# Dense feed-forward block: up products with the weights stationary and the tokens moving, results feature-major, no transposes of them

## The reference, cut to what matters

```python
D_MODEL, SEQ, D_FF = 1024, 256, 2816

def swiglu(u, w1, w3, w2):                 # u: 256 x 1024
    return (jax.nn.silu(u @ w1) * (u @ w3)) @ w2

# w1, w3: 1024 x 2816 (the two up products), w2: 2816 x 1024 (the down product)
```

## Time and profile before

| what | value |
|---|---|
| median of 3 runs | 2342.64 us (2339.24 to 2343.55) |
| span of the profiled execution | 2338.5 us |
| the profiled execution's own time beside its span | not listed; the shortest timed run is 0.7 us above the span |
| TensorE busy | 2098.2 us, 90% of the span |
| ScalarE, VectorE, GpSimd busy | 16%, 21%, 5% |
| the dense feed-forward (first up matmul to first matmul of what follows) | 357.23 to 598.87 us |

### The profile page before, as it was taken

One profiled execution on the slowest core, in us unless ns is written; L12 is line 12 of the kernel. 1 busy time (PEld: TensorE's weight loads), 2 busy tenths in 40 slices (PEclk: granted clock), 3 DMA queues, 4 the chain that ended last, 5 costly groups with the idle time before them and its releaser, 6 DMA issues. The chain is left out here.

```text
span 2338.5 us, 29578 instructions
## 1 busy us (share of the span) xinstructions
PE 2098.2 (90%) x12194; PEld 954.0 (41%) x12194; DVE 499.3 (21%) x1278; ACT 379.3 (16%) x878; POOL 116.4 (5%) x275
## 2 busy tenths in 40 slices
PE   5999998999999899999999999687798879879886
PEld 2574543444676343222222222154432328443232
DVE  2043841000159220000000011012311122131113
ACT  2022431000341321000000010022110010121011
POOL 2000000000000000000000000000000000000000
PEclk9999999999999999999999999887899899889999
DMA  9231359342673579999999999940899982079993
GB/s 319 93 123 45 136 182 329 134 146 90 238 266 132 219 280 362 412 407 398 408 402 412 404 406 411 373 151 0 326 422 422 422 314 73 36 317 422 422 418 148
DMA packets 192023, 644.22 MB, mean 275 GB/s; under 512 B 11635, under 2 KB 44875, under 8 KB 156043
## 3 DMA queue, kind: packets, MB, share of 16 engines
q1 hardware_dynamic: 165440, 469.92, 52.7%
q0 software_dynamic: 25824, 172.09, 18.1%
q10 hardware_dynamic: 619, 0.23, 0.0%
HBM read 641.15 MB, written 1.05 MB: 275 GB/s over the span
## 5 line engine op out<-in xcount | busy, mean ns | idle before, releaser
L1366 PE MATMUL bank<-ring,wide 128*32 128x512 f32 x3520 | 412.2, 598 | 22.2 <-DMA ring<-in_l_moe_w 20.6
L1403 PE MATMUL bank<-dreg,RB 128*32 128x512 f32 x2592 | 312.2, 601 | 7.4 <-DMA dreg<-in_l_moe_w 4.6
L1366 PEld LDWEIGHTS bank<-ring,wide 128*32 128x32 f32 x3520 | 108.6, 110 | 276.3 <-issue 245.1
L1349 PE MATMUL bank<-ring,wide 128*32 128x512 f32 x1472 | 189.0, 631 | 28.7 <-DMA ring<-in_w_up 27.3
L974 PE MATMUL bank<-wide,ring 128*128 128x256 f32 x832 | 182.1, 381 | 0.6 <-ACT wide L1808 0.6
L2945 DVE TENSOR_TENSOR H<-SG,bank 128x256 f32<-128x256 f32 x82 | 34.7, 423 | 689.6 <-ACT SG L2057 689.6
L974 PEld LDWEIGHTS bank<-wide,ring 128*128 128x128 f32 x832 | 158.5, 191 | 24.1 <-issue 2.2
L964 PE MATMUL bank<-ring,wide 128*128 128x512 f32 x352 | 158.2, 609 | 1.1 <-DMA ring<-in_w_kv 0.9
L1403 PEld LDWEIGHTS bank<-dreg,RB 128*32 128x32 f32 x2592 | 79.5, 110 | 190.7 <-issue 180.5
L1273 PE MATMUL bank<-ring,wide 128*128 128x512 f32 x352 | 154.6, 592 | 0.9 <-ACT wide L1808 0.9
L2972 DVE TENSOR_TENSOR TOK<-bank,TOK 128x512 f32<-128x512 f32 x84 | 57.9, 692 | 307.7 <-PE bank L1425 164.4
(11 more groups left out here) (445 smaller groups left out, 1617.7 us busy)
## 6 DMA issues: line engine op xcount, KB each, us to landing
ring<-in_l_moe_w SPq DMA_DIRECT2D x120, 1024.0 KB, 16.1
dreg<-in_l_moe_w POOLq DMA_DIRECT2D x88, 1024.0 KB, 8.5
dreg<-in_w_down POOLq DMA_DIRECT2D x64, 1024.0 KB, 12.8
ring<-in_w_gate SPq DMA_DIRECT2D x56, 1024.0 KB, 14.9
ring<-in_w_up SPq DMA_DIRECT2D x56, 1024.0 KB, 18.8
ring<-in_l_mod_w SPq DMA_DIRECT2D x24, 2048.0 KB, 8.2
ring<-in_l_moe_w SPq DMA_DIRECT2D x40, 768.0 KB, 12.7
ring<-in_l_ffn_w SPq DMA_DIRECT2D x22, 1024.0 KB, 10.0
```

The costliest lines, as they stand in the source:

```text
L1349: mm = pe.matmul(banks[r % 2][32 * g:32 * g + 32, :].rearrange("p (w n) -> p w n", w=2), tokens_of(m.order[i][0], c, k), w, start=k == 0, ...
L1366: mm = pe.matmul(banks[r % 3][32 * g:32 * g + 32, :].rearrange("p (w n) -> p w n", w=2), tokens_of(m.order[i][0], c, k), quads[:, s, :, k ...
L1403: mm = pe.matmul(banks[4 + 2 * m.lane(m.unit(m.order[i][0])) + h][32 * g:32 * g + 32, :], HQ[:, r % 4, j, 32 * q:32 * q + 32], dring[:, i ...
```

## The change

The up products swap their operands. A step is now one piece of work for all 256 tokens: with a 128x128 piece of the weights stationary and the 256 columns of `T1` moving, a matmul gives 128 features by 256 tokens. Four such groups of 8 matmuls fill two banks: the gate in bank `first`, the up part in bank `first + 1`. Steps alternate between banks 0, 1 and banks 2, 3. The result is feature-major, as the down product needs it, so the two transposes, ScalarE's copy and the two semaphores `turned_h` and `hidden_turned` go. ScalarE takes one silu of 128x512 per step, as soon as the gate's bank is full; VectorE multiplies 128x512 and writes to `H` in even steps, to `HT` in odd ones. `SG`, `H` and `HT` keep their memory and are seen as 512 columns. The down products of step st - 1 (8 matmuls, both token tiles) now follow the up products of step st. SyncE's code is not touched.

```diff
+                def up(st):
+                    s, first = st % RING, 2 * (st % 2)
+                    pe.wait_ge(sem(f"pair_in{s}"), 32 * (st // RING + 1))
+                    if st >= 2:
+                        pe.wait_ge(sem("hidden"), st - 1)
+                    for w in range(2):
+                        for j in range(2):
+                            for k in range(KC):
+                                operand_chunk(k, st == w == j == 0)
+                                m = pe.matmul(banks[first + w][:, j * T:(j + 1) * T], ring[:, s, k, (2 * w + j) * P:(2 * w + j + 1) * P],
+                                              T1[:, k, :], start=k == 0, stop=k == KC - 1)
                         m.then_inc(sem("upped"), 1)
...
+                def down(st):
+                    s = st % RING
+                    pe.wait_ge(sem(f"down_in{s}"), 16 * (st // RING + 1))
+                    pe.wait_ge(sem("hidden"), st + 1)
+                    for t in range(TT):
                         for j in range(2):
                             for n in range(2):
-                                m = pe.matmul(banks[4 + 2 * t + n][:, :], HT[:, t, j, :], dring[:, s, j, n * NCH:(n + 1) * NCH],
+                                m = pe.matmul(banks[4 + 2 * t + n][:, :], hidden_cols[st % 2][:, j * T + t * P:j * T + (t + 1) * P],
+                                              dring[:, s, j, n * NCH:(n + 1) * NCH],
                                               start=st == 0 and j == 0, stop=st == NSTEP - 1 and j == 1)
                         m.then_inc(sem("down_done"), 1)
-                    if 1 <= i <= nu:
-                        t = (i - 1) % TT
-                        pe.wait_ge(sem("hidden"), i)
-                        if i >= 3:
-                            pe.wait_ge(sem("hidden_turned"), i - 2)
-                        for j in range(2):
-                            m = pe.transpose(banks[2 + t][:, j * P:(j + 1) * P], H[:, t, j * P:(j + 1) * P], ident[:, :])
-                        m.then_inc(sem("turned_h"), 1)
+
+                for st in range(NSTEP):
+                    up(st)
+                    if st:
+                        down(st - 1)
+                down(NSTEP - 1)
...
+            for st in range(NSTEP):
+                act.wait_ge(sem("upped"), 2 * st + 1)
+                if st:
+                    act.wait_ge(sem("hidden"), st)
+                act.activation(silu_cols, banks[2 * (st % 2)][:, :], ACT.Silu).then_inc(sem("silued"), 1)
...
+            for st in range(NSTEP):
+                dve.wait_ge(sem("silued"), st + 1)
+                dve.wait_ge(sem("upped"), 2 * st + 2)
+                if st >= 2:
+                    dve.wait_ge(sem("down_done"), TT * (st - 1))
+                dve.tensor_tensor(hidden_cols[st % 2], silu_cols, banks[2 * (st % 2) + 1][:, :], ALU.mult).then_inc(sem("hidden"), 1)
```

More of the change, by code:

```diff
@@ L459, in two_blocks @@
         HT = sb("HT", [P, 2, 2, P])
+        silu_cols = SG[:, :, :].rearrange("p a n -> p (a n)")
+        hidden_cols = (H[:, :, :].rearrange("p a n -> p (a n)"), HT[:, :, :, :].rearrange("p a j n -> p (a j n)"))
         pairs = ring[:, :, :, :].rearrange("p s (w k) n -> p s w k n", w=2)
@@ L1259, in dense_ffn @@
             def dense_ffn():
[L1262 to L1274, removed]
-                        m.then_inc(sem("upped"), 1)
[L1276 to L1281, removed]
+                def up(st):
[9 more added lines that the diff above has]
+                                              T1[:, k, :], start=k == 0, stop=k == KC - 1)
+                        m.then_inc(sem("upped"), 1)
```

## The result

The changed kernel took 2325.0 us (median of 6 runs, 2317.43 to 2332.0) against 2343.1 us (6 runs, 2339.24 to 2347.48). The ratio is 0.9930, with a 95% interval of 0.9912 to 0.9947. The forecast was 2328.6 us and 14.0 us less. The profiled execution has a span of 2328.0 us, 10.5 us less than the one of before and 3.5 us more than the 2324.5 forecast for it. It belongs to a run of 2329.6 us, 4.6 us above the changed kernel's own median, so its span understates the gain.

A forecast was written before the change was run, and what follows sets the result against it. TensorE's own work was taken to bound the feed-forward; 4.84 + 8.49 + 1.44 + 0.20 - 0.8 - 0.2 = 13.97 us less, so 2342.64 - 14.0 gives 2328.6 us. The range was 2322 to 2337 us.

The forecast's parts named there:

- What bounds the stage: Feed-forward: TensorE's own work sets its length, busy 235.3 of 241.7 us, not the weights' supply or small engines.
- Transposes: Feed-forward units on TensorE: 22 transpose pairs of 0.22 us go, saving 4.84 us.
- The wait and the slow clock behind it: Before the first down product: 5.48 us idle for down weights and 3.01 us at half clock go, 8.49 us.
- Up products: Feed-forward up matmuls: 704 records of 256 columns at 0.2158 us, weight loads hidden, cost 0.8 us more.
- Start: First up group: TensorE may catch up with ScalarE's chunks, costing 0.2 us, between 0 and 0.9.
- Waits at the end: Last down units: waits for ScalarE's transpose copies (0.73 + 0.71 us) and the last unit's extra 0.20 us go.
- Rival C: Up products: weight loads from a ring slot being filled are not hidden, adding 48 us, time 2377; chance 4%.
- Handed on whole: Behind the feed-forward: later loads move with the chain, so the 14 us reach the end whole.
- within 3 us: Sign to check: the stretches behind the feed-forward stay as long as before to 3 us.

The follow-up runs named there:

- the late load: Changed kernel with SyncE issuing the first step's down weights last of the first four: stage 236.40 us, median 2329.95 us, ratio 0.9956.
- the second set: The changed kernel timed again without further edits: stage 227.65 us, median 2323.64 us, ratio 0.9924.
- the early load: Changed kernel with the first down weights issued behind the second pair of up weights: stage 227.65 us, median 2324.65 us, ratio 0.9926.
- the early table: Changed kernel with a one-column square root on ScalarE behind the last silu, loading its function table early: median 2322.70 us, ratio 0.9917.
- the control: The kernel before, unchanged, timed as if it were another kernel: stage 241.72 us, median 2341.39 us, ratio 0.9997.

## Why the prediction was right, point by point

- *What bounds the stage*: TensorE's own work. Confirmed: it is busy for all of it. The forecast of the stage (227.6 us) came out at 227.65 by this mechanism and not by luck: its two large terms were tested one by one.
- *Transposes* (4.84 us): 4.83 measured by putting them back.
- *The wait and the slow clock behind it* (8.49 us): 8.47 measured in the kernel before by issuing one load earlier. The margin was put at 1.4 us and is 1.0 in one trace and 1.4 in the other. That it decides is shown by the late load (+8.75 us).
- *Up products* (+0.8 us): 0.07 us per 64 records, and 0.9 us of up work more in the kernel before with its matmuls cut. The number was right; the reason given for it was not. The prediction said that a load of 0.191 us is hidden under a pitch of 0.2158 "with 25 ns to spare". At 128 columns records with a load each lie 0.112 us apart, so a load costs at most that, and at least 0.1 us was to spare.
- *Start* (+0.2 us): the first 128 records take 384.23 - 356.53 = 27.70 us where 2 x 13.81 = 27.62, so 0.08.
- *Waits at the end* (1.44 and 0.20 us): gone; the last down records run at 6.87 us a step and the next job follows. Not tested apart from the rest, but with the other terms measured, 13.99 - 4.83 - 8.47 + 0.7 + 0.1 = 1.5 us is left for them.
- *Rival C*, the one on the slower side, was rightly held unlikely, but neither its reason nor its price holds. It named the transfers that fill the ring, and the first 128 records take 27.70 us, 0.216 each, at a DMA share of 1.07 (357 to 384). What sets line 1322 apart is the stride of its stationary operand, which the prediction did not name: a stride of 8 gives the same loads (337 ns, 334 there). The worst stride costs 16.8 us, not 48, which even then would have been 2.8 us slower than before and no measurable change.
- *Handed on whole*: the experts' loads on SyncE's queue start at 785.01 and 781.89 in the two traces of the changed kernel, 12.5 and 15.6 us before the 797.51 of before. Behind the stage the program takes 1739.7 and 1737.8 us in the traces of before, 1743.8 and 1737.3 in those of the changed kernel. The first of these is 4.1 us longer, past the prediction's "within 3 us", the second is not; the two differ by more from each other than from before, so neither a loss nor a further gain is shown. The prediction called 880 to 1480 bound by transfers; its own row has TensorE busy for 587.72 of 600 us at full clock beside a DMA share of 1.02, so the row doesn't say which of the two bounds it. The medians moved by 18.1 and, in the second set, 18.0 us, 4 more than the stage. That the total of 2325.0 fell inside the range owes nothing to a term for this: the prediction had none, and the range was wide enough. The medians of the variants stray from what their stages say as well, mostly downwards: the late load by 6.5 us, the kernel before with cut matmuls by 3.7, the early load by 2.7, the early table by 2.4, 44 transposes by 2.3, the early load in the kernel before by 1.2, and upwards stride 2 by 0.6 and 128 columns by 5; the control by 0.2. I found no stretch that is shorter in the changed kernels' traces. The clock's falls at single waits are large enough for it (2 us each), but that they are rarer in the changed kernels was not shown. This stays open.

## What to carry to other kernels

Before crediting a new layout with a gain, ask which of its waits another order of the loads would have removed as well: here 8.5 of 14 us were one down load issued 20 us later than it could be, and the new layout hides it by 1.0 to 1.4 us only. A stage without a wait in its timeline can be forecast by counting records and pitches to 0.1 us; take the pitch from a row of the same shape and never from a weight load's length. And where a short wait may or may not bring the clock down, compare the stage across traces, not the totals, and look at more than two traces before saying what makes it fall.

## What the runs showed of the hardware that I had not expected

- Weight loads overlap one another. At 128 moving float32 columns loads of 0.192 us follow each other every 0.112 us, so a 512-column moving operand (0.429 us a record) can be swapped for two of 256 (0.216 each) at 0.5% more time, or for four of 128 (0.112 each) at some 4% more.
- What a load costs rises with the stride of the stationary operand by a step between 2 and 4: length 0.190, 0.196, 0.330 and 0.337 us at strides 1, 2, 4 and 8 of float32, and pitches of 0.216, 0.216, 0.235 and 0.240 us with 256 columns moving.
- At one and the same short wait the clock falls in three traces (waits of 1.14 to 1.38 us) and stays up in nine (0.88 to 1.21 us); the spans outside the stage differ by 7 us between two traces of one kernel.
